# Second block's feed-forwards: 256-column inputs, normalised ahead, from the seventh unit on

## What is computed

```python
def _modulate(h, shift, scale):
    return h * (1 + scale[:, None, :]) + shift[:, None, :]

def _swiglu(h, w_in, w_out):
    a, b = jnp.split(h @ w_in, 2, axis=-1)
    return (jax.nn.silu(a) * b) @ w_out
...
    for l in range(DEPTH):
        mod = c_act @ ada_w[l] + ada_b[l]
        sh1, sc1, gt1, sh2, sc2, gt2, sh3, sc3, gt3 = jnp.split(mod, N_MOD, axis=-1)

        h = _modulate(_rmsnorm(x, ffn1_norm[l]), sh1, sc1)
        x = x + FFN_RES * gt1[:, None, :] * _swiglu(h, ffn1_w_in[l], ffn1_w_out[l])
...
        h = _modulate(_rmsnorm(x, ffn2_norm[l]), sh3, sc3)
        x = x + FFN_RES * gt3[:, None, :] * _swiglu(h, ffn2_w_in[l], ffn2_w_out[l])
```

## Time and profile before

| what | us |
|---|---|
| three executions, median | 3090.3 |
| the profiled execution | 3091.63 |
| its span on the core | 3089.9 |
| TensorE busy in it | 3001.7 |
| VectorE, ScalarE, GpSimd busy | 2103.8, 971.1, 703.3 |
| L2486, busy sum of the three products (they overlap) | 405.9, 401.5, 400.5 |
| L2510, the same | 198.1, 196.8, 196.8 |

### The profile page before, as it was taken

The page is one execution under the profiler, slowest core; times in us unless marked ns, Lnnn a source line. Parts: engine busy times, 40 slices in busy tenths (PEclk is TensorE's granted clock), DMA queues, the critical chain, the costliest instruction groups (busy, mean ns, idle before and its releaser), DMA issues.

```text
span 3089.9 us, 45987 instructions
## 1 busy us (share of the span) xinstructions
PE 3001.7 (97%) x18914; PEld 2685.3 (87%) x18914; DVE 2103.8 (68%) x2247; ACT 971.1 (31%) x1027; POOL 703.3 (23%) x614
## 2 busy tenths in 40 slices
PE   8999999999999999999998899999999999999999
PEld 5778889988887888878888699899989999999999
DVE  4864359867279543795637776687797868768764
ACT  2112222212131121221215343343544343354443
POOL 1220100124113010130201022231462313228110
PEclk9999999999999999999999999999999999999999
DMA  7543235322245333353623387586547868755564
GB/s 266 191 150 96 95 87 200 137 96 82 96 127 192 126 94 103 123 204 109 204 99 123 107 268 251 172 279 225 200 158 247 258 204 274 239 188 198 158 188 154
DMA packets 501665, 522.74 MB, mean 169 GB/s; under 512 B 15732, under 2 KB 433830, under 8 KB 501478
## 3 DMA queue, kind: packets, MB, share of 16 engines
q1 hardware_dynamic: 498536, 513.76, 50.4%
q0 software_dynamic: 2944, 6.32, 1.0%
HBM read 518.97 MB, written 1.05 MB: 168 GB/s over the span
## 4 chain that ended last, share of the span: by engine, by line
PE 77%; DVE 15%; ACT 3%; issue 3%; DMA 2%; POOL 0%; SPq 0%; DVEq 0%; ACTq 0%
PE ps L2309 22%; PE ps L2396 15%; PE ps L2486 14%; PE ps L2337 7%; PE ps L2510 7%; DVE wl L1293 4%; DVE acc L1247 3%; PE ps L2374 2%; DVE lnp L1247 2%; ACT wh L864 2%; PE ps L2353 2%; PE ps L2423 1%; DVE mraw L1254 1%; PE ps L2757 1%; PE ps L2789 1%
## 5 line engine op out<-in xcount | busy, mean ns | idle before, releaser
L1293 DVE TENSOR_TENSOR wl<-wraw,wh 128x2048 fp32r<-128x2048 f32 x341 | 825.6, 2421 | 513.1 <-ACT wh L864 508.5
L864 ACT ACTIVATE wh<-wraw 128x2048 fp32r<-128x2048 f32 x341 | 652.7, 1914 | 904.1 <-PE ps L2396 380.0
L2309 PE MATMUL ps<-xh,wh 128*128 128x512 f32 (+1 forms) x1504 | 553.7, 368 | 15.6 <-DVE wl L1293 15.4
L2309 PE MATMUL ps<-xh,wl 128*128 128x512 f32 (+1 forms) x1504 | 549.7, 366 | 0.0
L2309 PE MATMUL ps<-xl,wh 128*128 128x512 f32 (+1 forms) x1504 | 549.4, 365 | 0.0
L2486 PE MATMUL ps<-xh,wh 128*128 128x258 f32 x1408 | 405.9, 288 | 10.9 <-DVE wl L1293 7.1
L704 POOL CAST hh<-ht 128x256 f32 (+1 forms) x176 | 143.5, 816 | 1170.0 <-DVE ht L1685 845.8
L2486 PE MATMUL ps<-xh,wl 128*128 128x258 f32 x1408 | 401.5, 285 | 0.0
L2486 PE MATMUL ps<-xl,wh 128*128 128x258 f32 x1408 | 400.5, 284 | 0.0
L1247 DVE SCALAR_TENSOR_TENSOR acc<-mraw,svec,acc 128x1024 f32<-128x1024 f32 x259 | 347.7, 1362 | 6.1 <-DVE prea L1332 0.4
L2309 PEld LDWEIGHTS ps<-xh,wh 128*128 128x128 f32 x1504 | 284.1, 189 | 63.4 <-DVE wl L1293 17.1
(11 more groups left out here) (443 smaller groups left out, 5456.3 us busy)
## 6 DMA issues: line engine op xcount, KB each, us to landing
wraw<-in_ffn_w_in SPq DMA_DIRECT2D x352, 512.0 KB, 4.8
wraw<-in_ffn_w_out SPq DMA_DIRECT2D x176, 512.0 KB, 4.2
mraw<-in_ada_w SPq DMA_DIRECT2D x72, 1024.0 KB, 6.3
mraw<-in_w_mod SPq DMA_DIRECT2D x64, 1024.0 KB, 6.7
wraw<-in_gmlp_w_in SPq DMA_DIRECT2D x48, 512.0 KB, 4.2
wraw<-in_mix_w_in SPq DMA_DIRECT2D x48, 512.0 KB, 4.5
wraw<-in_gmlp_w_out SPq DMA_DIRECT2D x24, 512.0 KB, 3.9
first_w<-in_w_mod SPq DMA_DIRECT2D x8, 1024.0 KB, 11.0
```

What stands on the lines that cost most here:

```text
L864: act.activation(wh[:, slot], wraw[:, slot], ACT.Copy).then_inc(whi_done, 1)
L1293: dve.tensor_tensor(wl[:, slot], wraw[:, slot], wh[:, slot].bitcast(F32), ALU.subtract)\
L2309: m = pe.matmul(ps[:, bank, 0:width], a, b, start=k == p == 0, stop=k == KD - 1 and p == 2)
```

## The change

Units 0 to 5 stay (`EARLY = 6`). For units 6 to 21 a second input is made, `yh` and `yl`, of 256 columns: VectorE's `scaled` multiplies each of the eight groups of `x` by its factors and by `rstd_b` into `sq` (four in iteration 0, four in iteration 1), ScalarE adds the shift and rounds to `yh` (Identity, in its iterations 0 and 1, behind the SiLU), and VectorE's `low_scaled` writes the rest to `yl` (iterations 1 and 2). TensorE waits for them at unit 6. Behind these units `take` is gone: ScalarE's SiLU and VectorE's product read PSUM, and the pair is released by `product_late`, which stands behind the split of the unit after next. `late_in` lies behind `xl2` and reaches 304 values into `hh`'s place, so the hidden tensors of all four begin at 304, with no step; sub-layer 5's step is 0 now. The order in which the modulation's weights are loaded (`FF_MODS`) is the same in both kernels.

```diff
--- before.py
+++ after.py
@@ -19,8 +19,9 @@
 TT = T // P
 XW, XS = T + 2, T + 16
 ONE_AT = 48
-INNER_AT = {5: 0, 6: 48, 8: 0, 9: 48, 11: 0}
-INNER_STEP = {5: 4, 6: 0, 8: 16, 9: 0, 11: 4}
+INNER_AT = {5: 0, 6: 304, 8: 304, 9: 304, 11: 304}
+INNER_STEP = {5: 0, 6: 0, 8: 0, 9: 0, 11: 0}
+EARLY = 6
 DEPTH = 2
 D_FF = 2816
 KF = D_FF // P
@@ -238,6 +239,8 @@
         cg_t = wst_flat[0:32, 512:768]
         pool_term, dve_taps = wst_flat[:, 768:1024], wst_flat[:, 512:768]
         q2, k2 = (w[:, 1].rearrange("p (a b) -> p a b", a=4) for w in (gate, acc))
+        _, late_in = alias(("before_late", [P, 2 * KD * XS], F32), ("late_in", [P, 48 + 2 * KD * T], F32R))
+        yh, yl = (late_in[:, 48 + i * KD * T:48 + (i + 1) * KD * T].rearrange("p (k q) -> p k q", k=KD) for i in range(2))
         sb("place_of_inputs", [P, 2 * KD * 2 * T])
 
         hh, hl = alias(("hh", [P, 12 * 512], F32R), ("hl", [P, 12 * 512], F32R))
@@ -341,6 +344,7 @@
         x_ready, xt_ready = sem("x_ready"), sem("xt_ready")
         hi_ready, lo_ready = sem("hi_ready"), sem("lo_ready")
         sq_act, sq_pool, sq_summed = sem("sq_act"), sem("sq_pool"), sem("sq_summed")
+        y_scaled, y_high, y_ready = sem("y_scaled"), sem("y_high"), sem("y_ready")
         hidden, ss_ready, rb_ps, rb_ready, a_ready = sem("hidden"), sem("ss_ready"), sem("rb_ps"), sem("rb_ready"), sem("a_ready")
         t_ready = sem("tmp_ready")
         fin_tr, out_ready = sem("fin_tr"), sem("out_ready")
@@ -436,6 +440,10 @@
 
             half = INNER_STEP[s["i"]] // 2
             return bass.ds(idx * (T + half) + (INNER_AT[s["i"]] - j % 2 * half), T)
+
+        def late(s):
+
+            return (s["n_sg"] - subs[B2]["n_sg"]) // KF
 
         def ff_mods(idx):
 
@@ -948,11 +956,21 @@
                             act.activation(rstd_b, ps[:, 6, 0:T], ACT.Copy).then_inc(rb_ready, 1)
                         if i < KF:
                             pair = i % 2
-                            act.wait_ge(a_ready, b0 + i + 1)
+                            if i < EARLY:
+                                act.wait_ge(a_ready, EARLY * late(s) + i + 1)
+                            else:
+                                act.wait_ge(w_used, u0 + i + 1)
                             if b0 + i > 1:
                                 act.wait_ge(hidden, b0 + i - 1)
-                            act.activation(sg[:, pair, T:2 * T], sg[:, pair, 0:T], ACT.Silu, bias=shift_col[:, pair, 0:1])\
-                                .then_inc(sg_ready, 1)
+                            if i < EARLY:
+                                act.activation(sg[:, pair, T:2 * T], sg[:, pair, 0:T], ACT.Silu, bias=shift_col[:, pair, 0:1])\
+                                    .then_inc(sg_ready, 1)
+                            else:
+                                act.activation(sg[:, pair, T:2 * T], ps[:, 2 * pair, 0:T], ACT.Silu).then_inc(sg_ready, 1)
+                        for n in range(4 * i, 4 * i + 4) if i < 2 else ():
+                            j = order_in(s)[n]
+                            act.wait_ge(y_scaled, 8 * late(s) + n + 1)
+                            act.activation(yh[:, j], sq[:, j], ACT.Identity, bias=modc[:, s["i"] % 2, 0, 0, j:j + 1]).then_inc(y_high, 1)
                 elif s["kind"] == "ffn":
                     W = T * len(s["streams"])
                     m0, u0 = 0, s["n_unit"]
@@ -1645,19 +1663,47 @@
                         steps.link(dve.tensor_tensor(sq[:, 0:4], sq[:, 0:4], sq[:, 4:8], ALU.add))
                         dve.tensor_tensor(sq[:, 0:2], sq[:, 0:2], sq[:, 2:4], ALU.add).then_inc(sq_summed, 1)
 
+                    def product_late(i):
+                        pair = i % 2
+                        dve.wait_ge(sg_ready, s["n_sg"] + i + 1)
+
+                        dve.wait_ge(h_ready, s["n_h"] + i)
+                        dve.tensor_tensor(ht[:, pair, 0:T], ps[:, 2 * pair + 1, 0:T], sg[:, pair, T:2 * T], ALU.mult).then_inc(hidden, 1)
+                        dve.wait_ge(hidden, KF * late(s) + i + 1)
+                        dve.sem_inc(pair_free, 1)
+
+                    def scaled(n):
+
+                        j = order_in(s)[n]
+                        dve.scalar_tensor_tensor(out=sq[:, j], in0=xT[:, j], scalar=prea[:, 0, j:j + 1], in1=rstd_b,
+                                                 op0=ALU.mult, op1=ALU.mult).then_inc(y_scaled, 1)
+
+                    def low_scaled(n):
+
+                        j = order_in(s)[n]
+                        dve.wait_ge(y_high, 8 * late(s) + n + 1)
+                        dve.scalar_tensor_tensor(out=yl[:, j], in0=sq[:, j], scalar=modc[:, s["i"] % 2, 0, 0, j:j + 1],
+                                                 in1=yh[:, j].bitcast(F32), op0=ALU.add, op1=ALU.subtract).then_inc(y_ready, 1)
+
                     squares_summed()
                     split_next(u0)
                     mean_square(s)
                     for i in range(32):
-                        if 0 < i < KF:
+                        if 0 < i < EARLY:
                             take(i)
                         if i < 31:
                             split_next(u0 + i + 1)
                         if i == 0:
                             dve.wait_ge(rb_ready, s["n_sqp"] // 3 + 1)
                             take(0)
-                        if i < KF:
+                        if i < EARLY:
                             product(i)
+                        elif i < KF:
+                            product_late(i)
+                        for n in range(4 * i - 4, 4 * i) if i in (1, 2) else ():
+                            low_scaled(n)
+                        for n in range(4 * i, 4 * i + 4) if i < 2 else ():
+                            scaled(n)
                         if i == 1 and s["i"] == B2:
                             mod_end(s, 2)
                         if nxt:
@@ -2481,9 +2527,13 @@
                             for n, k in enumerate(order):
                                 if i == r == 0:
                                     pe.wait_ge(lo_ready, 8 * s["m"] + n + 1)
+                                if i == EARLY and r == 0:
+                                    pe.wait_ge(y_ready, 8 * late(s) + n + 1)
                                 at = slice(k * CW + r * P, k * CW + (r + 1) * P)
-                                for p, (a, b) in enumerate(parts(wh[:, slot, at], wl[:, slot, at], now[0][:, k, 0:XW], now[1][:, k, 0:XW])):
-                                    m = pe.matmul(ps[:, 2 * pair + r, 0:XW], a, b, start=n == p == 0, stop=n == KD - 1 and p == 2)
+                                width = XW if i < EARLY else T
+                                high, low = (w[:, k, 0:width] for w in (now if i < EARLY else (yh, yl)))
+                                for p, (a, b) in enumerate(parts(wh[:, slot, at], wl[:, slot, at], high, low)):
+                                    m = pe.matmul(ps[:, 2 * pair + r, 0:width], a, b, start=n == p == 0, stop=n == KD - 1 and p == 2)
                             if i == 1 and r == 0:
                                 rows_of_factors(s)
                         m.then_inc(w_used, 1)
```

## The result

The changed kernel takes 3125.8 us (median of four executions, 3118.7 to 3127.6), the kernel before 3089.8: a ratio of 1.0111, 95% interval 1.0093 to 1.0129. Slower, as foreseen, but by 36 us where 10 were; the range ended at 3108. The profiled execution took 3118.7 us (span 3117.0), 27 us more than the profiled one of before.

A forecast was written before the change was run, and what follows sets the result against it. TensorE, busy 97% of the span, was taken as the bound. Costs 14.7 + 8.8 = 23.5 us less gains 7.1 + 1.3 + 5.4 = 13.8 make 9.7 us slower: 3101.3, given as 3100; range 3088 to 3108.

The forecast's parts named there:

- The walk through the start: Units 1 to 5 of each feed-forward: added instructions delay the splits; 4.1 us in three, 2.4 in the last, 14.7 us cost.
- S(4): Start of unit 4 on TensorE in the feed-forward of 2336 us, claimed to come 2.35 us late.
- S(5): Start of unit 5 on TensorE in the same feed-forward, claimed to come another 1.7 us late, together 4.1 us.
- S(3): Start of unit 3 on TensorE in the feed-forward of 2336 us, at 2358.6, claimed to be kept.
- The wait in the first output unit: Each output's start, ahead of the fifth bank: TensorE waits 2.2 us for unit 21's pair, four times, 8.8 us cost.
- The folds: Ends of modulation sections: PSUM reads leave VectorE's queue, so unit 11 starts 0.3 us earlier; six folds gain 1.8 us.
- The paces: Late units at 117.8 ns gain 5.3 us; outputs resuming at the quicker pace after their wait gain 5.4 us.
- The place of the hidden tensors: Outputs of the second and last feed-forward: the new place of their input gains 1.1 and 0.2 us, sum 1.3.
- dearer starts and no quicker pace: Rival, chance 0.17: starts cost 18 us instead of 14.7, none of the outputs' 5.4 us gain comes; 3108 us.
- Rivals 1: Quicker pace of 113.4 ns from unit 6 or the first pause; gains 25.4 us against 23.5; 3088 us, chance 0.17.
- 3: Rival: the output's wait is hidden or doesn't come; 3097 us, or 3091 with quicker pace behind the folds; chance 0.13.
- 4: Rival: only the column count sets the matmul pace, as the skill's rule has it; 3111 us, chance 0.05.

The follow-up runs named there:

- fillers: Matmuls of no use put into the times in which TensorE waits, in the changed kernel; 3111.5 us, ratio 1.0062 to the kernel before.

## Why the prediction was wrong in size

Its direction and its two main costs were right. Two steps failed most: the walk priced four operations in a row as if GpSimd stood still (most of 6.5 us), and the effect of a pause on the clock was put at nothing (about 6 us). Step by step (foreseen, then measured, for four feed-forwards):

- **The walk through the start, 14.7, then 21.2.** The rows of the walk were right, its order too. The mis-sized term is the group of four operations: 0.40 us each, but 0.67 us more per group beside GpSimd. The text held this for the upper end "if operations with two SBUF inputs meet GpSimd's cast", 18 us, and took the lower, though the product that wakes GpSimd stands directly ahead of each group. With it: S(4) 2.35 + 1.3 late, S(5) and the rest 4.1 + 2.0 = 6.1, measured 6.0 in the feed-forward of the walk. That S(3) is kept was wrong by 0.5 us for the same reason: in the first and third feed-forward, whose first group is undisturbed, S(3) is kept. The rule was cited and not followed to its number.
- **The wait in the first output unit, 2.2, then 2.35, 2.35, 2.67 and 2.12:** 9.5 us for 8.8. The mechanism and the size were right; releasing earlier took it away.
- **The clock behind the pause, never considered, then 4.5 us in the output starts,** about 1.5 at a unit 19 and 0.5 at a unit 4; in other executions more. It is the largest step left out, and the text called the pause's effect "good" alone. In these units the trace of before has only pauses of up to 1.3 us, none with a slow stretch behind. But elsewhere in the program it held the price: TensorE idles for 2.3 us or more twelve times, and within 6 us of ten of them the granted clock reads 0.50; of the six idle times of 1.4 to 1.8 us none is followed by it. One of the shortest, 2.33 us, and what came behind it:

```profile
887.59 0.36 PE L2291 MATMUL ps<-xh,wh 128*128 128x256 f32 x1 [2.33 <-ACT xh L903]
...
889.40:892.80 3.40, 3.40 (x18) 0.50 0.00 0
```

- **The folds, a gain of 1.8, then a loss of 2.6.** Taking the PSUM reads away did save 0.73 us. Against it stand, in the feed-forward of 2345 us: 0.54 us from the split's end to TensorE's start, for product and release, 0.06 before; 0.63 us from the product's start to the modulation's, as the release waits for the product's end, 0.40 before; and 3.13 us instead of 2.61 for its two operations. Together they make the fold 0.5 us longer. The first was foreseen (0.42 and a step), the two others not. The third is again a meeting with GpSimd, and which side pays turned round: before, GpSimd's cast took 1.27 us and VectorE's operations their usual time; now the cast takes 0.40, ahead of them, and they run beside the subtraction. That the order of starts decides this is likely, not shown.
- **The paces.** Entry at 117.8 was right in all four. The late units gained 7.1 (units 6 to 10, 11 to 18, 19 to 22; the slow unit 19 and small waits are in it) where 5.3 were foreseen, since the folds led to 113.3 in four of six places, which the text had excluded. The outputs gained 3.7 for 6.3. In the first feed-forward the wait ended at 117.8 again. In the next two the units ran quicker up to the wait ahead of unit 27, which is there before as well, and that wait grew from 0.5 and 0.6 to 0.9 us: nearly half of the gain ahead of it is lost. The 240 matmuls of the text should be 216 (half a unit and four), 0.3 us in three. That a pace changes only where TensorE has paused was wrong: one matmul of another kind is enough. The place of the hidden tensors was exact.

Sum of the misses: 6.5 + 2.5 + 5.7 + 2.6 = 17.3 us, the distance from 9.7 to 27.0. Of the 36 us between the medians the other 9 lie outside the two traces: the profiled execution of the changed kernel was 7 us under its median, that of the kernel before 2 us over.

Of the rivals, "dearer starts and no quicker pace" had the right cause for its larger part, but at 18 us it was under the 21.2. Rivals 1, 3 and 4 are out: the costs came, the waits came, and paces differ at one width.

## What to carry to other kernels

Instructions put into idle time of an engine need more than a gap of the right length: ask what the instruction ahead of them wakes elsewhere, and price them with both engines at work. Spread mostly in twos over the real gaps, the same 24 instructions cost nothing. An instruction that frees a buffer belongs ahead of the long one, not behind it: this order alone was worth 20 us. Price a pause of the bounding engine as its length plus what follows it, and look for that price in all of the trace, not only beside the change; before moving a step look at every queue that waits for its semaphore.

## What the runs showed of the hardware

- **Pauses and the clock.** In the twelve traces without fillers, units 2 to 31 of these feed-forwards have 81 pauses of 0.8 to 1.9 us, none with a stretch at 1.2 GHz behind it; 35 of 2.0 to 2.6 us, 20 with one; 22 of 2.7 to 3.8 us, 21 with one. So between 2.0 and 2.6 us the length alone doesn't decide. The stretch begins at the restart or about a microsecond later. Its slow steps add 1.1 to 1.7 us, and 2.5 or 2.6 in three traces behind the longest pause, 3.8 us.
- **Places and paces.** At 256 columns, weights loaded anew for every matmul: 120.0 ns with the moving input at a round place, 118.4 to 118.6 with rows of 272 values, and 117.8 or 113.3 at 48 values past a round place. Only the last has two. It can change between them at a pause, at one or two matmuls of another kind, or at a wait as short as 0.03 us, and at others like them it stays. The formula for the step in the Trainium skill (TensorE: Matmul & The Clock Gate, Back-to-back issue gap) has only the number of columns in it, and the page gives it for isolated matmuls; here the place moved the step by 6.7 ns at the same columns. What decides which of the two comes is open.
- **A slow engine can be free.** Two units 4 partly at half the clock took 8.08 and 8.07 us, and 8.08 at the full one: VectorE set the next unit's start.
